# Decays of the sample sequences' states: from VectorE, behind the state sums, to GpSimd, before them

## The chip, the cores and the metric

One core of a Trainium2 chip. The metric is device time in microseconds (us) of one execution, the median of several executions of the same program. Two numbers of a profiled execution come beside it: the span of the trace, and that execution's own device time.

## What is computed

One inference step of a two-layer decoder trunk, for a prompt of 256 tokens and for 8 sample sequences of 4 new tokens each. Each layer projects the normalised input once and feeds three groups of heads: sparse attention with an indexer that picks 256 of 2052 keys (A), dilated window attention (C), and a Mamba-2 scan (B). Their gated outputs are joined and projected back.

What matters here is the recurrent state of B. For each of the 8 sample sequences and 6 heads it is a 64 by 128 matrix, and a step makes of it (cut from the reference):

```python
chunk_decay = jnp.exp(acs[:, :, -1, :])
def step(h, inp):
    st, dec = inp
    return h * dec[:, :, None, None] + st, h
h_final, h_in = lax.scan(step, h0, (states.swapaxes(0, 1), chunk_decay.swapaxes(0, 1)))
```

The old state times its decay, plus the sum over the new tokens. The new state is an output; the token outputs of the layer use the old one.

## The kernel before, in words

Everything lies feature by token: 256 prompt tokens and 32 sample tokens are 288 columns, `T`. The engines run programs of their own, written out by hand in the order in which they issue, and wait on semaphores. A layer has these stages: eight projection tiles; 16 pairs of cache pages with eight more projection tiles between them; the search for the 256th largest score, bit by bit, on VectorE (`compare`, `settle`, 32 rounds) with a small matmul of TensorE in each round (`bit_count`) and projections, the scan and the window attention between the rounds; then the softmax of the sparse attention, 32 groups of value pages (`value_group`) with projections, prompt attention and the state sums between them; then eight output tiles.

**State.** The tile `state` (in the profile `phased`, whose memory it shares) holds the 8 sequences' states, 384 columns each. SyncE loads it (line 501). `sample_offsets` (1368) reads the old states on TensorE. ScalarE writes the decays into `ebc` in `ssd_exp(h)` (836 and 837), once for each of the 6 heads, and counts `ebc_ready`. `state_sums(i)` (1405) puts the new parts of sequences 4i to 4i+3 into PSUM banks, and `state_out(b)` on VectorE (1988) waits for bank `ss{b}`, multiplies the state by the decays (1991), waits for itself, adds the bank (1994) and so gives the bank free. Sequences 0 to 3 are followed by `prompt_state_out` and three `top8_round`, then 4 to 7. GpSimd stores all states once the last bank is free (639).

**GpSimd's program around the change.** After the last rope and its stores come `masked(0)` and `masked(1)` (569), then `consumed(*RING[40:44])`, then `y_gated(t)` for three tiles (590), then `consumed(*RING[44:60])`. `consumed` reloads slots of the ring of eight `kv` buffers: for each item it waits for TensorE to have read the slot and issues four transfers (438), GpSimd for the odd places, SyncE for the even ones. Items 40 to 43 of the ring are window values and items 48 and up are the value pages: `consumed(*RING[40:44])` loads places 49 and 51, and the next call begins with 53 and 55.

**Who waits for `y_gated`.** It multiplies the scan's output by its gate, on a tile whose memory the transposed probabilities take over next. So ScalarE waits for all three before the first exponential of the sparse softmax:

```python
act.wait_ge(S["sexp_in"], nth(L, "sexp_in", 1))
act.wait_ge(S["ki_out"], nth(L, "ki_out", 16))
act.wait_ge(S["y_ready"], nth(L, "y_ready", 3))
sparse_exp(0)
```

These are lines 905 to 908; the exponential itself is line 875. `sexp_in` comes from VectorE (2182), behind the masking of the scores (2174). Behind `sparse_exp` come TensorE's transposes (1006, called at 1501), ScalarE's `sparse_turned` (881), and the value groups.

Of the kernel before, what the change touches and what calls it, by code (L numbers as in the profile page):

```python
# [18 lines left out]
ALU = mybir.AluOpType  # L19
# [8 lines left out]
NB, NQ = 8, 4  # L28
# [72 lines left out]
RING = ([("page", n) for n in range(KITEMS)] + [("window", n) for n in range(2 * NB)] + [("value", n) for n in range(NGRP)])  # L101
# [45 lines left out]
def bank_plan():  # L147
# [59 lines left out]


PER = {
    "rstd_ready": 1, "sq_ready": 8, "sq_used": 5, "y_normed": 5, "y_pooled": 3, "z_gated": 1, "xw_ready": 8, "xn_free": 7, "xn_ready": 8, "roped": 15, "shuffled": 7, "ssum_ready": 1, "root_ready": 1,  # L210
    "qs_ready": 1, "relu_used": 1, "prelu_used": 8, "cnt_ready": NCOUNT + 1, "cin_used": 7, "tanhed": 7, "conved": 7,
    "qz_ready": 1, "qcz_zero": 1, "so_sel": 1, "qcz_ready": 6, "qcbd_ready": 6, "mask_ready": 1, "sexp_in": 1, "sexp": 5, "px_ready": 1,
    "pexp_in": 2, "pexp": 2, "pprob": 2, "pv0_done": 1, "dexp_in": 2, "dexp": 2, "dprob": 2,
# [9 lines left out]
def build(nc, a):  # L223

    plan, _ = bank_plan()
    with ExitStack() as ctx:
        def sb(name, shape, dt=F32):
            return ctx.enter_context(nc.sbuf_tensor(name, shape, dt))
# [52 lines left out]
        state = phasedf.rearrange("p (b n) -> p b n", b=NB)  # L281
# [39 lines left out]
        ebc = sb("ebc", [P, 6, 10])  # L321
# [9 lines left out]
        S = {name: ctx.enter_context(nc.semaphore(name))  # L331
             for name in ("x_in0", "x_in1", "ptab_in", "prm_in", "cst_in", "const_in", "ones_set", "zeroed", "act_chain", "dve_chain", "pool_chain", "y_out",
                          *[f"w_in{n}" for n in range(WSLOTS)], *[f"kv_in{n}" for n in range(NKV)], *PER)}
# [3 lines left out]
        def bank_of(use):  # L337
            return bank[plan[use][0]]

        def filled(use):  # L340
            return S[f"filled{plan[use][0]}"]

        def drained(use):
            return S[f"drained{plan[use][0]}"]

        def nth(layer, what, n=None):

            if n is None:
                what, n = f"filled{plan[what][0]}", plan[what][1] + 1
            return layer * PER[what] + n  # L350
# [38 lines left out]
        def each(ap, m):  # L389

            return ap.unsqueeze(2).to_broadcast([ap.shape[0], ap.shape[1], m])
# [50 lines left out]
        def after(engine, kind, layer, item):  # L442


            at = PLACE[item] + NKV
            layer, at = (layer, at) if at < len(RING) else (layer + 1, at - len(RING))
            if layer < DEPTH and at % 2 == (kind == mybir.EngineType.Pool):
                load_item(engine, kind, layer, at)
# [78 lines left out]
        def _(pool):  # L527
            POOL = mybir.EngineType.Pool
            chain = Chain(S["pool_chain"])
# [4 lines left out]
            for L in range(DEPTH):  # L534
# [14 lines left out]
                def consumed(*items):  # L549

                    for item in items:
                        after(pool, POOL, L, item)
# [14 lines left out]
                def masked(i):  # L567

                    pool.tensor_scalar(xwb[:, i, :], xws[:, 2, :], C("bm", i, i + 1), None,
                                       ALU.mult).then_inc(S["xwb_ready"], 1)  # L570
# [61 lines left out]
                keep(*STAGE_KEEPS[L][4], "proj24")  # L632
                masked(0)
                masked(1)
                consumed(*RING[40:44])
                for t in range(3):
                    y_gated(t)
                consumed(*RING[44:60])
# [963 lines left out]
        def _(dve):  # L1602
# [25 lines left out]
            for L in range(DEPTH):  # L1628
                chain = Chain(S["dve_chain"])
                tt_, ts_, stt = dve.tensor_tensor, dve.tensor_scalar, dve.scalar_tensor_tensor  # L1630
# [357 lines left out]
                def state_out(b):  # L1988

                    dve.wait_ge(filled(f"ss{b}"), nth(L, f"ss{b}"))  # L1990
                    tt_(state[:, b, :].rearrange("p (h n) -> p h n", h=6), state[:, b, :].rearrange("p (h n) -> p h n", h=6),
                             each(ebc[:, :, 2 + b], 64), ALU.mult).then_inc(chain.next(), 1)
                    dve.wait_ge(S["dve_chain"], chain.n)
                    tt_(state[:, b, :], state[:, b, :], bank_of(f"ss{b}")[:, 0:384], ALU.add).then_inc(drained(f"ss{b}"), 1)

                def prompt_state_out():
# [198 lines left out]
                for b in range(4):  # L2195
                    state_out(b)
# [3 lines left out]
                for b in range(4, NB):  # L2200
                    state_out(b)
# [216 lines left out]
```

## Time and profile before

| | us |
|---|---|
| median of 3 executions | 609.94 |
| lowest, highest | 609.93, 610.36 |
| the profiled execution, its own device time | 606.36 |
| span of its trace | 604.6 |

The span is 1.76 us shorter than the profiled execution's own time, which in turn is 3.58 us below the median of the others. Starts are in us from the start of the span. PE is TensorE, DVE VectorE, ACT ScalarE, POOL GpSimd; a number in square brackets behind a timeline row is the idle time of that engine just before it and what ended it. In rows of waits the three numbers are the total in us, how often, and the longest in us; in rows of busy time by stretch, behind the length come TensorE, its weight loads, VectorE, ScalarE and GpSimd, then the granted clock as a share of full speed, the DMA engines' share and GB/s. Layer 0 takes the first 297 us or so, layer 1 the rest; the stretch of the change is at 169 to 222 us and again at 460 to 513 us.

### The profile page before, as it was taken

Reading aid. Unit: us, or ns where it says so; the run is one execution under the profiler, and the core shown is the slowest. Engines: PE = TensorE matmul, PEld = TensorE weight load, DVE = VectorE, ACT = ScalarE, POOL = GpSimd, SP = SyncE. Lnnn points to the kernel's source line nnn. Section 1 sums busy time; section 2 is a strip of 40 time slices with the busy share of each in tenths; the row PEclk is TensorE's granted clock in tenths of the full one; section 3 lists DMA queues with packets and bytes.
Section 4 is the critical chain, followed back from the end, with each engine's and each line's share of the span. In section 5 each row is a group of like instructions: output and inputs, shape, how many; then the busy total and the mean of one; then the engine's idle time right before and its main releaser. Section 6 shows DMA issues by size and latency. Waiting matters only on the chain.

```text
span 604.6 us, 13428 instructions
## 1 busy us (share of the span) xinstructions
PE 555.4 (92%) x4656; PEld 385.6 (64%) x4656; DVE 354.7 (59%) x1081; ACT 175.5 (29%) x457; POOL 241.6 (40%) x433
## 2 busy tenths in 40 slices
PE   4999999999999987999899999999999988799980
PEld 3776655677776654667677565557777755566760
DVE  4864655667776683534267563657678648553223
ACT  3013522112234342641001351311223344264110
POOL 0506642457327446261011474334843464631201
PEclk9999999999999997999999999999999999999996
DMA  8978999999999999798969999999999999993582
GB/s 328 318 279 296 369 368 386 414 355 354 397 395 348 335 307 359 245 347 295 376 208 370 296 362 372 374 417 360 368 367 379 383 336 315 345 322 98 201 302 78
DMA packets 75108, 198.37 MB, mean 328 GB/s; under 512 B 11585, under 2 KB 44770, under 8 KB 70946
## 3 DMA queue, kind: packets, MB, share of 16 engines
q1 hardware_dynamic: 53570, 99.50, 46.7%
q0 software_dynamic: 21472, 98.03, 44.1%
q8 instruction: 37, 0.61, 0.4%
q14 instruction: 29, 0.24, 0.1%
HBM read 189.33 MB, written 52.00 MB: 399 GB/s over the span
## 4 chain that ended last, share of the span: by engine, by line
PE 73%; DMA 9%; DVE 5%; SPq 5%; ACT 5%; issue 2%; DVEq 0%
PE bank L960 69%; DMA kv<-in_kk 6%; SPq L438 4%; PE bank L1006 3%; DMA w<-in_w 3%; ACT shared L765 1%; ACT srow L875 1%; ACT shared L748 1%; DVE shared L1838 1%; DVE shared L1821 1%; DVE st L1827 1%; DVE srow L2174 1%; SPq L434 0%; DVE xn L2256 0%; DVE shared L1785 0%
## 5 line engine op out<-in xcount | busy, mean ns | idle before, releaser
L960 PE MATMUL bank<-xn,w 128*128 128x288 f32 x1120 | 293.8, 416 | 8.2 <-DMA w<-in_w 8.2
L960 PEld LDWEIGHTS bank<-xn,w 128*128 128x128 f32 x1120 | 206.6, 191 | 77.0 <-issue 22.4
L438 POOL DMA_DIRECT2D kv<-in_kk x128 | 68.9, 539 | 91.4 <-PE bank L960 44.2
L438 POOL DMA_DIRECT2D kv<-in_vv x128 | 68.8, 539 | 90.5 <-PE bank L960 49.5
L701 ACT ACTIVATE pt<-bank 128x288 f32<-128x288 f32 x48 | 19.6, 409 | 191.9 <-PE bank L960 191.9
L960 PE MATMUL bank<-pt,w 128*128 128x288 f32 x256 | 64.1, 408 | 1.2 <-DMA w<-in_w 1.2
L960 PEld LDWEIGHTS bank<-pt,w 128*128 128x128 f32 x256 | 48.1, 190 | 15.4 <-DMA w<-in_w 2.0
L541 POOL DMA_DIRECT2D out_keep<-in_buf x48 | 25.0, 527 | 81.1 <-PE bank L960 79.3
L1696 DVE TENSOR_SCALAR_CACHE_REDUCE hit<-sc,tb 128x516 bf16<-128x516 f32 x62 | 46.5, 750 | 2.2
L960 PE MATMUL bank<-kv,qz 128*32 128x256 f32 x512 | 34.3, 385 | 0.0
L960 PE MATMUL bank<-kv,pt 128*32 128x256 f32 x512 | 33.5, 391 | 0.0
L2242 DVE TENSOR_TENSOR x<-x,bank 128x288 f32<-128x288 f32 x16 | 7.3, 454 | 40.0 <-PE bank L960 40.0
L1669 DVE COPY tails<-cin 128x3 f32<-128x3 f32 x14 | 4.8, 344 | 44.1 <-ACT cin L699 41.9
L960 PE MATMUL bank<-pt 64*128 64x128 f32 (+3 forms) x168 | 27.5, 351 | 0.0
L670 ACT ACTIVATE phased<-x 128x288 f32<-128x288 f32 x24 | 10.4, 442 | 58.5 <-DVE x L2242 52.7
L960 PEld LDWEIGHTS bank<-pt 64*128 64x128 f32 (+2 forms) x168 | 18.7, 193 | 11.6 <-issue 10.6
L1675 DVE SCALAR_TENSOR_TENSOR cacc<-cin,prm,cacc 128x312 f32<-128x312 f32 x42 | 22.8, 544 | 1.5
L1707 DVE TENSOR_SCALAR tb<-bank 128x1 int32<-128x1 f32 x62 | 9.6, 155 | 23.8 <-PE bank L960 23.1
L431 POOL DMA_DIRECT2D kv<-in_dil x16 | 8.7, 547 | 35.5 <-PE bank L960 35.3
L960 PEld LDWEIGHTS bank<-kv,pt 128*32 128x32 f32 x512 | 14.4, 111 | 12.1 <-issue 4.7
L960 PEld LDWEIGHTS bank<-kv,qz 128*32 128x32 f32 x512 | 13.4, 109 | 11.8 <-issue 6.3
L960 PE MATMUL bank<-kv,shared 128*32 128x128 f32 x576 | 18.6, 275 | 0.0
(262 smaller groups left out, 737.6 us busy)
## 6 DMA issues: line engine op xcount, KB each, us to landing
w<-in_w SPq DMA_DIRECT2D x86, 512.0 KB, 8.6
out_keep<-in_buf POOLq DMA_DIRECT2D x16, 2044.0 KB, 13.9
kv<-in_kk SPq DMA_DIRECT2D x128, 160.0 KB, 8.4
kv<-in_kk POOLq DMA_DIRECT2D x128, 160.0 KB, 5.8
kv<-in_vv SPq DMA_DIRECT2D x128, 128.0 KB, 4.8
kv<-in_vv POOLq DMA_DIRECT2D x128, 128.0 KB, 4.8
kv<-in_dil SPq DMA_DIRECT2D x16, 576.0 KB, 11.4
kv<-in_dil POOLq DMA_DIRECT2D x16, 576.0 KB, 8.1
```

The lines of the kernel that those rows point to most:

```text
L431: engine.dma_start(kv[:, s, 0:9 * P], a["dil"][layer, item // NB * NB + SEQ_ORDER[item % NB]]).then_inc(S[f"kv_in{s}"], 16)
L438: engine.dma_start(kv[:, s, r * rec:(r + 1) * rec], a["kk" if what == "page" else "vv"][bass.ds(page + layer * N_POOL, 1)].rearrange("o p ...
L541: pool.dma_start(a[f"keep{g}"][bass.ds(layer, 1), b], a[f"buf{g}"][bass.ds(layer, 1), b, 4 * 256:], max_dma_last_dim=COPY_ROW).then_inc(S[ ...
L670: act.activation(squares[:, k % 2, 0:T], x[:, k, :], ACT.Square).then_inc(S["sq_ready"], 1)
L701: act.activation(ptile(i), src[:, 0:T], fn).then_inc(use, 1)
L748: act.activation(psa[:, i, 0:nk], psa[:, i, 0:nk], ACT.Exp, bias=st8[:, 1, i:i + 1], accum_out=st8[:, 2, i:i + 1]).then_inc(S["pexp"] if i ...
L960: return pe.matmul(out, lhsT, rhs, start=start, stop=stop, skip_group_check=True, **k)
L1006: return pe.transpose(out, in_, ident(n))
L1675: stt(out=o, in0=cin[:, n % 2, j:j + COUT], scalar=prmc(L, "cw", 4 * n + j), in1=o, op0=ALU.mult, op1=ALU.add).then_inc(S["cin_used"] if j ...
L1696: ts_(hit[:, :], sc[:, :], old.bitcast(F32), 0.0, ALU.is_ge, ALU.add, accum_out=cnt[:, 0:1]).then_inc(S["cnt_ready"], 1)
L1707: ts_(tb[:, 2:3], src[:, 0:1], float(TOPK_S), float(bit), ALU.is_lt, ALU.mult).then_inc(drained(f"count{n}"), 1)
L2242: tt_(x[:, m, :], x[:, m, :], src[:, 0:T], ALU.add).then_inc(drained(f"out{m}"), 1)
```

## The change

Two places. On GpSimd eight multiplications of a state by its decays are put between `masked(1)` and `y_gated(0)`: four before `consumed(*RING[40:44])`, four behind it, with one wait for the sixth `ebc_ready` ahead of them. On VectorE `state_out` loses its multiplication and the wait for it, and waits for `decayed` instead. Nothing is computed that was not computed before.

```diff
@@ PER
+    "decayed": 8,
@@ GpSimd, layer L
                 masked(0)
                 masked(1)
-                consumed(*RING[40:44])
+                pool.wait_ge(S["ebc_ready"], nth(L, "ebc_ready", 6))
+                for b in range(NB):
+                    if b == 4:
+                        consumed(*RING[40:44])
+                    pool.tensor_tensor(state[:, b, :].rearrange("p (h n) -> p h n", h=6), state[:, b, :].rearrange("p (h n) -> p h n", h=6),
+                                       each(ebc[:, :, 2 + b], 64), ALU.mult).then_inc(S["decayed"], 1)
                 for t in range(3):
                     y_gated(t)
                 consumed(*RING[44:60])
@@ VectorE, state_out(b)
                     dve.wait_ge(filled(f"ss{b}"), nth(L, f"ss{b}"))
-                    tt_(state[:, b, :].rearrange("p (h n) -> p h n", h=6), state[:, b, :].rearrange("p (h n) -> p h n", h=6),
-                             each(ebc[:, :, 2 + b], 64), ALU.mult).then_inc(chain.next(), 1)
-                    dve.wait_ge(S["dve_chain"], chain.n)
+                    dve.wait_ge(S["decayed"], nth(L, "decayed", b + 1))
                     tt_(state[:, b, :], state[:, b, :], bank_of(f"ss{b}")[:, 0:384], ALU.add).then_inc(drained(f"ss{b}"), 1)
```

## Rows read from the trace of the kernel before

**Rows 1.** the page, busy time by engine and granted TensorE clock in 40 slices

```profile
PE 555.4 (92%) x4656; PEld 385.6 (64%) x4656; DVE 354.7 (59%) x1081; ACT 175.5 (29%) x457; POOL 241.6 (40%) x433
...
PEclk9999999999999997999999999999999999999996
```

**Rows 2.** instructions on the tile phased (state), VectorE: ns min/median/max

```profile
L1991 DVE TENSOR_TENSOR phased<-phased,ebc x16: 549/551/559, 206.4 to 511.1; 128x384 f32<-128x384 f32 x16
L1994 DVE TENSOR_TENSOR phased<-phased,bank x16: 553/553/555, 207.0 to 511.6; 128x384 f32<-128x384 f32 x16
```

**Rows 3.** everything TensorE waited for, 190 to 230 us: first and last of 4

```profile
PE bank L1006 <- ACT srow L875: 1.9, 3, 0.7
...
PE bank L1006 <- ACT vtok L741: 0.3, 1, 0.3
```

**Rows 4.** VectorE timeline, layer 0: start us, us, what

```profile
230.46 0.17 DVE L1829 TENSOR_SCALAR st<-st 128x2 f32<-128x2 f32 x1
```

**Rows 5.** ScalarE timeline, both layers

```profile
171.48 0.17 ACT L837 ACTIVATE ebc<-bank 128x8 f32<-128x8 f32 x1
...
231.92 1.28 ACT L765 ACT_TABLE_LOAD   x1
...
484.46 0.72 ACT L875 ACTIVATE srow<-srow,st 128x512 f32<-128x512 f32 x1 [1.86 <-DVE st L2182]
```

**Rows 6.** GpSimd timeline, layer 0: start us, us, what [idle before]

```profile
130.95 2.40 POOL L587 TENSOR_TENSOR xws<-xw,dec 128x384 f32<-128x384 f32 x3
...
184.42 2.32 POOL L438 DMA_DIRECT2D kv<-in_vv  x4 [12.74 <-issue]
187.16 2.29 POOL L438 DMA_DIRECT2D kv<-in_vv  x4 [0.42 <-issue]
189.97 2.30 POOL L594 TENSOR_TENSOR pt<-pt 128x288 f32<-128x288 f32 x3 [0.52 <-ACT pt L902]
192.22 4.27 POOL L438 DMA_DIRECT2D kv<-in_vv  x8
```

**Rows 7.** ScalarE's own wait at line 907: count, ns, first and last start

```profile
L907 ACTq EVENT_SEMAPHORE  x2: 38/38/38, 192.3 to 483.4; - x2
```

**Rows 8.** chain that ended last, layer 0: start us, us, what

```profile
193.46 0.17 DVE st L2182
...
193.65 0.82 ACT srow L875 x2
...
198.60 13.19 PE bank L960 x120
...
277.84 9.81 DMA w<-in_w
```

**Rows 9.** GpSimd timeline, layer 1

```profile
478.01 2.31 POOL L438 DMA_DIRECT2D kv<-in_vv  x4 [0.42 <-issue]
481.08 2.30 POOL L594 TENSOR_TENSOR pt<-pt 128x288 f32<-128x288 f32 x3 [0.75 <-ACT pt L902]
```

**Rows 10.** costliest GpSimd groups by shape: busy us, mean ns

```profile
L569 POOL TENSOR_SCALAR xwb<-xws,const 128x384 f32<-128x384 f32 x4 | 5.0, 1247 | 0.1
...
L654 POOL TENSOR_TENSOR xn<-xn,rstd 128x288 f32<-128x288 f32 x3 | 2.9, 978 | 24.3 <-DVE rstd L1613 24.3
```

**Rows 11.** landing times of the four GpSimd transfers of 192.22 to 194.3 us

```profile
DMA to landing us min/median/max: 4.9/5.1/5.7
```

**Rows 12.** TensorE timeline, layer 1 and layer 0

```profile
489.35 2.80 PE L960 MATMUL bank<-kv,pt 128*32 128x256 f32 x48
...
526.50 0.87 PE L1006 MATMUL bank<-const,shared 128*128 128x128 f32 x6 [3.23 <-DVE shared L1838]
...
235.68 1.54 PE L1006 MATMUL bank<-const,shared 128*128 128x128 f32 x6 [3.23 <-DVE shared L1838]
```

**Rows 13.** one stretch of layer 0: length, busy times, granted clock, DMA share

```profile
236.20:242.00 5.80, 5.80 (x37) 3.33 (x37) 0.80 (x2) 1.15 (x3) 3.13 (x7) 0.54 1.05 377
```

**Rows 14.** VectorE at line 2256, beside line 654: ns min/median/max

```profile
L2256 DVE SCALAR_TENSOR_TENSOR xn<-x,fnw,rstd x5: 503/1037/1046, 593.0 to 596.3; 128x288 f32<-128x288 f32 x5
```

More of the change, by code:

```diff
@@ L209 @@
 PER = {
-    "rstd_ready": 1, "sq_ready": 8, "sq_used": 5, "y_normed": 5, "y_pooled": 3, "z_gated": 1, "xw_ready": 8, "xn_free": 7, "xn_ready": 8, "roped": 15, "shuffled": 7, "ssum_ready": 1, "root_ready": 1,
+    "rstd_ready": 1, "sq_ready": 8, "sq_used": 5, "y_normed": 5, "y_pooled": 3, "z_gated": 1, "decayed": 8, "xw_ready": 8, "xn_free": 7, "xn_ready": 8, "roped": 15, "shuffled": 7, "ssum_ready": 1, "root_ready": 1,
     "qs_ready": 1, "relu_used": 1, "prelu_used": 8, "cnt_ready": NCOUNT + 1, "cin_used": 7, "tanhed": 7, "conved": 7,
```

## The prediction

> **What bounds the kernel now.** The page comes first: TensorE is busy 92% of the span, VectorE 59%, GpSimd 40% [rows 1]. So time taken from VectorE counts only where TensorE stands still for it, and time put on GpSimd only where somebody waits for GpSimd. The question is who waits in the two stretches of the change, and it has to be asked twice, once for what is removed and once for what is added.
>
> **What is removed: worth nothing.** VectorE loses 16 multiplications of 551 ns, eight in each layer, 8.8 us of busy time in all [rows 2]. Between 190 and 230 us TensorE waited four times in kind, every time for ScalarE: for the exponentials, for the squares and roots of the group norm, for evacuated tokens [rows 3]. It never waited for a bank that the states' additions give back, though they came with the multiplications ahead of them. Behind the states VectorE goes through the group norm to the maxima of the dilated scores, done at 230.46 + 0.17 = 230.63 us [rows 4]. The next user is ScalarE's exponential, and ScalarE itself is free only at 231.92, when TensorE's projection has been evacuated [rows 5]. So VectorE is 1.3 us early already, and after the change it is early by 2.2 us more (4 x 0.55, since the first four states and the last four are apart, with waits for TensorE between them). What hides the gain is ScalarE's order behind TensorE; without that cover each layer would gain at most 2.2 us. I take zero.
>
> **What is added, first four.** GpSimd's `masked(1)` ends at 184.42 - 12.74 = 171.68 us [rows 6]. The sixth `ebc_ready` comes from ScalarE's instruction of 171.48 + 0.17 = 171.65 [rows 5]. The new wait costs nothing. Behind it GpSimd is idle for 12.74 us, until TensorE has read the window values and places 49 and 51 can be reloaded. A multiplication has the very form of line 587, 128x384 with the decay broadcast; three of those took 2.40 us one behind the other, so 0.80 each [rows 6]. Four take 3.2 us and end near 175, more than 9 us before the reloads of 184.42. They cost nothing, and no DMA is late for them.
>
> **What is added, last four.** These stand behind the reload of place 51, which ends at 187.16 + 2.29 = 189.45 us, and ahead of `y_gated` [rows 6]. The three `y_gated` start at 189.97 and take 2.30 us; they had waited 0.52 us for ScalarE's gate. With 3.2 us of multiplications in front they start at 192.65 and end at 194.95, where they ended at 192.27.
>
> Who waits for that? ScalarE, at line 907, before the first exponential of the sparse softmax. Its wait there was over at 192.3 and 483.4 us, which is the moment at which `y_gated` ends [rows 7]. The exponential began at 193.65, behind VectorE's instruction of 193.46 + 0.17 = 193.63 [rows 8]. So `y_gated` had 1.38 us to spare in layer 0. Added are 3.20, less 0.52 of idle time filled, less 1.38: the exponential starts 1.3 us later. In layer 1 the reload ends at 478.01 + 2.31 = 480.32; `y_gated` waited 0.75 and ended at 483.38 [rows 9]; the exponential began at 484.46 [rows 5]. So 3.20 - 0.75 - 1.08 = 1.37, 1.4 us. This wait lies on the chain that ended last: exponential, transposes, and from 198.60 on 13.19 us of TensorE without a gap [rows 8]. VectorE's multiplications don't give it back, as they come only after it.
>
> A multiplication's price has two ends. The slowest GpSimd operation on 384 columns, `masked`, took 1.247 us [rows 10]; at that price each layer is 4 x 0.45 = 1.8 us worse. Below 0.77, what `y_gated` needs for 288 columns (2.30 / 3), it can't well go; that saves 0.1 per layer. I take 0.80, the same form in the same engine.
>
> VectorE's own time for the same form is 0.55 [rows 2], so GpSimd is 1.45 times slower. The Trainium skill speaks against such a move (GPSIMD Engine Reference, 4.1 Engine selection: two-input elementwise work belongs on VectorE, GpSimd being about twice as slow; 3.1 gives 1.96 times). An estimate by that figure would be 1.08 us each, and so 2.2 us more for both layers, 4.9 in all. The trace has the duration, so 1.45 stands.
>
> **Behind `y_gated` on GpSimd's queue** stand the reloads of places 53 and 55, which began at 192.22 [rows 6] and now begin near 194.95. Of the four transfers for 53 the last starts 1.6 us later and lands at most 5.7 us after that [rows 11]: at 199.5 before, at 202.3 now. TensorE reads that place in its sixth value group; six groups are 48 matmuls in 2.80 us [rows 12], so the sixth begins 2.3 us after 198.6, at 200.9, and with the delay at 202.2. It is a tie. I take zero here, with up to 0.8 us per layer as the bad end. SyncE's transfers depend on TensorE alone and move with it. The store of the states comes later than all of this and nobody on the chain waits for it. VectorE's new wait for `decayed` is over at 192.7 for the last state, and the first addition comes after 206 [rows 2].
>
> **Does the delay survive?** Near the end of layer 0 TensorE waits 9.81 us for weights [rows 8]. Their load is issued when output tile 0 is done, so it moves with TensorE, and I let the delay through. Layer 1 has no such wait behind the change.
>
> **The sum** is 1.3 + 1.4 = 2.7 us. Against the profiled execution's own 606.36 that is 609.1. The median is 3.58 us above that execution, and I add the sum to it: 609.94 + 2.7 = 612.6.
>
> **Rivals.**
> 1. **The clock.** In the one fall of the granted clock inside the span [rows 1], at 236.2 to 242.0, it was 0.54 over 5.80 us [rows 13], TensorE at its lower level of 1.2 GHz nearly throughout. It lost (1 - 0.54) x 5.8 = 2.7 us. Ahead of it TensorE had stood idle for 3.23 us; in layer 1 the same idle time had no fall behind it [rows 12]. So it is near the edge, and moving the idle times can turn it over. The change also lengthens an idle time, from the 0.7 us before the first transposes [rows 3] to 2.1. One fall more: 612.6 + 2.7 = 615.3, chance 0.12. One fewer: 609.9, no change, 0.11.
> 2. **Faster, by the same mechanism.** The unprofiled executions took 3.58 us more than the profiled one. If a second fall, behind the idle time that ends at 526.50, is part of that, then both falls can go when layer 0's idle time moves by 1.3 and layer 1's by 2.7: 612.6 - 5.4 = 607.2. It decides where neither idle time ends in a fall. For it speaks only that difference; against it, that both must go together. Chance 0.06.
> 3. **Engines in each other's way.** In the last stage three GpSimd multiplications of 288 columns took 978 ns instead of 770 [rows 10], and VectorE's instructions beside them 1037 instead of 503 [rows 14]. If the last four multiplications suffer like that, at 1.25 us each, the time is 612.6 + 3.6 = 616.2. Against it: beside them VectorE adds a PSUM bank to the scores, as it did beside `y_gated`, which ran undisturbed in 2.30 us [rows 6]. Chance 0.05. The Trainium skill has it as an exclusive lock (SBUF, "SBUF: two separate sides"): a VectorE instruction with two SBUF inputs and a GpSimd one that reads SBUF exclude each other. By that rule, the last stage agrees, and the scores' instructions, with one input in PSUM, don't count.
> 4. **Half of it is absorbed**, because the transfers behind layer 0's 9.81 us wait use the delay to land earlier: 611.3, chance 0.06.
> 5. **The change doesn't delay anything**, because the exponential waits for more than I see and `y_gated` has more to spare: 609.9, chance 0.04.
>
> **How the numbers follow.** The forecast, both layers late by 1.3 to 1.4 us, has 0.56; its own range is 612.3 to 614.2 (the tie of place 53 lost in both layers). A measurement of this kernel can tell 0.2% from no change, 1.2 us. Slower by more than that are the forecast, rivals 1 (one more), 3 and 4: 0.56 + 0.12 + 0.05 + 0.06 = 0.79. Within it: 0.11 + 0.04 = 0.15. Faster: 0.06. The range of 609.8 to 615.6 leaves out rivals 2 and 3, 0.11, and edges of the others.
>
> **What would show it.** After the change, ScalarE's first exponential should be released by GpSimd's line of `y_gated`, not by VectorE's line 2182, near 195.0 us and 1.3 us later than before; four multiplications of 0.80 us should lie at 171.7 to 175 and four at 189.5 to 192.7; TensorE's idle time before the first transposes should be 2 us; VectorE should show 8.8 us less busy time and as much more idle time, ended by TensorE and ScalarE. It is wrong if the exponential is still released by VectorE, if TensorE turns out to gain behind 217 us, or if the span moves while the exponentials don't.

## The result, and the profile after

The changed kernel takes 622.67 us (median of 6 runs, 619.60 to 627.91), the kernel before 609.78 in runs beside it (6 runs, 608.29 to 610.36). The ratio is 1.0222, 95% interval 1.0189 to 1.0255: slower by 12.9 us. The forecast was 612.6, with a range up to 615.6: right in sign, about five times too small in size. Medians here are of all executions; ratios and their intervals come from executions taken side by side and leave out those over 1.5% above the fastest of the same kernel, so a ratio isn't always the quotient of two medians. The profiled execution took 627.91 us, with a span of 626.2, so it is the slowest of the six; against the profiled execution of before it is 21.5 us longer, not 12.9.

The page of the changed kernel, busy time by engine and granted clock:

```profile
PE 566.1 (90%) x4656; PEld 391.5 (63%) x4656; DVE 357.8 (57%) x1065; ACT 176.0 (28%) x457; POOL 254.6 (41%) x449
...
PEclk9999999999997997999999999999999897999996
```

GpSimd has its 16 additional instructions and 13.0 us more [rows 1]. But VectorE, which lost 16 multiplications of 0.55 us, is busy 3.1 us *longer*. Something on VectorE has grown by 12 us. The timelines of the stretch in layer 0 show it; GpSimd first (start us, us, what, idle before):

```profile
172.88 3.28 POOL L639 TENSOR_TENSOR phased<-phased,ebc 128x384 f32<-128x384 f32 x4
...
190.38 0.54 POOL L438 DMA_DIRECT2D kv<-in_vv  x1 [0.35 <-issue]
190.93 3.22 POOL L639 TENSOR_TENSOR phased<-phased,ebc 128x384 f32<-128x384 f32 x4
194.12 2.28 POOL L594 TENSOR_TENSOR pt<-pt 128x288 f32<-128x288 f32 x3
```

and VectorE of the changed kernel:

```profile
190.12 0.43 DVE L2170 TENSOR_TENSOR hit<-hit,eqs 128x516 bf16<-128x516 bf16 x1
190.58 5.97 DVE L2172 TENSOR_SCALAR maskbf<-hit 128x516 bf16<-128x516 bf16 x1
```

This is the instruction that turns the result of the search into the additive mask of the scores (line 2169 in the listing of before, where the trace has it so):

```profile
189.43 0.30 DVE L2169 TENSOR_SCALAR maskbf<-hit 128x516 bf16<-128x516 bf16 x1
```

One instruction of 0.30 us takes 5.97, and 6.03 in layer 1. It begins 0.35 us before GpSimd's multiplications and ends at 196.55, 0.15 us after the last `y_gated`: it was shut out while GpSimd worked through all seven instructions (four multiplications, three `y_gated`). GpSimd itself isn't slowed, 3.22 us for four. In the kernel before, the mask began while the last transfer was being issued and ended at 189.73, in the 0.52 us in which GpSimd waited for ScalarE's gate [rows 6].

TensorE waits for the mask, and projects before the softmax only behind it. Its timeline in the changed kernel, layer 0 and layer 1:

```profile
190.26 1.24 PE L965 MATMUL bank<-xn,w 128*128 128x288 f32 x4
196.61 0.62 PE L965 MATMUL bank<-maskbf,bconst 32*128 32x512 bf16 x5 [5.11 <-DVE maskbf L2172]
197.16 5.51 PE L965 MATMUL bank<-xn,w 128*128 128x288 f32 x12
...
206.47 2.80 PE L965 MATMUL bank<-kv,pt 128*32 128x256 f32 x48
...
496.05 0.62 PE L965 MATMUL bank<-maskbf,bconst 32*128 32x512 bf16 x5 [5.16 <-DVE maskbf L2172]
496.60 5.97 PE L965 MATMUL bank<-xn,w 128*128 128x288 f32 x12
```

The same stretch before:

```profile
189.11 1.24 PE L960 MATMUL bank<-xn,w 128*128 128x288 f32 x4
190.28 0.40 PE L960 MATMUL bank<-maskbf,bconst 32*128 32x512 bf16 x5
190.61 3.18 PE L960 MATMUL bank<-xn,w 128*128 128x288 f32 x12
...
198.53 2.80 PE L960 MATMUL bank<-kv,pt 128*32 128x256 f32 x48
```

From the four matmuls to the value groups it was 198.53 - 189.11 = 9.42 us and is 206.47 - 190.26 = 16.21: 6.8 us more. In layer 1 it is 7.3 more. Three terms: the wait, 5.1 us; twelve matmuls at a lower granted clock, 5.51 instead of 3.18, 2.3 us; and 0.7 us less waiting for the exponentials, which now lie beside the slow projection. Both layers give 14.1 us. The rest of the 21.5 is mostly further falls of the clock: in the last 120 us, from the value groups of layer 1 on, the granted clock was 0.91 where it had been 0.95, and that stretch is 4.6 us longer. The two PEclk rows show them (2 slices under nine tenths before, the last one among them, and 5 after), and they differ from execution to execution. The changed kernel was profiled once more (e9_after_again): 618.56 us in that execution, 12.2 above the profiled one of before, and there the two stretches come to as much. Its TensorE timeline in layer 0:

```profile
191.55 1.24 PE L965 MATMUL bank<-xn,w 128*128 128x288 f32 x4
197.88 0.62 PE L965 MATMUL bank<-maskbf,bconst 32*128 32x512 bf16 x5 [5.10 <-DVE maskbf L2172]
198.43 4.86 PE L965 MATMUL bank<-xn,w 128*128 128x288 f32 x12
...
207.09 2.80 PE L965 MATMUL bank<-kv,pt 128*32 128x256 f32 x48
```

207.09 - 191.55 = 15.54, so 6.1 more than before; in layer 1 it was 5.9 more, together 12.0.

Last, what the forecast rested on. ScalarE's exponential in the changed kernel:

```profile
200.20 0.72 ACT L880 ACTIVATE srow<-srow,st 128x512 f32<-128x512 f32 x1 [7.25 <-DVE st L2185]
```

It is still released by VectorE, which the prediction had named as a sign of being wrong. `y_gated` ended at 196.40, which is 5.5 us behind the last transfer issue where it had been 2.8: 2.7 us later, as forecast. But the exponential was not due before 200.20.

### The profile page after: what moved, and what is told of

Read it like the earlier page. It is cut to its first block and busy times, and to the rows that moved or that the text cites. A ratio compares the mean times of both kernels' runs of the same rounds, so it can differ in the third digit from the quotient of the medians.

```text
span 626.2 us, 13440 instructions
## 1 busy us (share of the span) xinstructions
PE 566.1 (90%) x4656; PEld 391.5 (63%) x4656; DVE 357.8 (57%) x1065; ACT 176.0 (28%) x457; POOL 254.6 (41%) x449
## 5 line engine op out<-in xcount | busy, mean ns | idle before, releaser
L965 PE MATMUL bank<-xn,w 128*128 128x288 f32 x1120 | 299.6, 422 | 8.1 <-DMA w<-in_w 8.1
L965 PEld LDWEIGHTS bank<-xn,w 128*128 128x128 f32 x1120 | 210.3, 195 | 80.5 <-issue 23.9
L965 PE MATMUL bank<-kv,pt 128*32 128x256 f32 x512 | 35.6, 411 | 0.0
L675 ACT ACTIVATE phased<-x 128x288 f32<-128x288 f32 x24 | 10.4, 441 | 58.9 <-DVE x L2245 53.4
L965 PE MATMUL bank<-kv,ea 64*32 64x128 f32 x512 | 14.4, 281 | 5.2 <-DMA kv<-in_kk 4.0
```

Of the source, the lines that this page charges most:

```text
L675: act.activation(squares[:, k % 2, 0:T], x[:, k, :], ACT.Square).then_inc(S["sq_ready"], 1)
L965: return pe.matmul(out, lhsT, rhs, start=start, stop=stop, skip_group_check=True, **k)
```

## The experiments

All ratios are to the kernel before on the same chip. Its medians there were 609.37 us (17 runs) beside e1 to e4, 610.28 (23 runs) beside e5 to e7 and 608.98 (11 runs) beside e8 and e9. A kernel with one run is told with the one run of before beside it.

**e1_gaps: the same order, but with pauses.** Each of the last four multiplications waits for its predecessor's semaphore.

```diff
                     if b == 4:
                         consumed(*RING[40:44])
+                    if b >= 4:
+                        pool.wait_ge(S["decayed"], nth(L, "decayed", b + 1))
```

> The changed kernel, but GpSimd waits on its own count behind each of the last four multiplications, so that no two of its instructions there follow each other without a pause. Theory G (VectorE's bf16 mask instruction, 0.30 us before and 5.97 us after the change, can't begin as long as GpSimd runs instructions back to back, and begins at the first pause): it ends behind the first multiplication, within 1.2 us of its start; TensorE's wait for it (5.1 and 5.2 us) falls below 0.9 us; what is left is the late y_gated, so 612.5 to 614 us. Rival H (the mask instruction shares its time with GpSimd's instructions for as long as these run, pauses or not): it still lasts over 5 us and the time is that of the changed kernel, 619 to 628 us.

The wait is for the count that the multiplication ahead has given. Measured: 616.21 us (6 runs), ratio 1.0144 [1.0098, 1.0190]. Instructions on the tile `maskbf` and TensorE's timeline:

```profile
L2174 DVE TENSOR_SCALAR maskbf<-hit x2: 1357/1389/1421, 189.7 to 482.4; 128x516 bf16<-128x516 bf16 x2
```

```profile
196.96 1.95 PE L1013 MATMUL bank<-const,srow 128*128 128x128 f32 x8 [2.38 <-ACT srow L882]
```

The four multiplications took 3.60 instead of 3.22 us, and the mask got in behind the first of them: 1.4 us instead of 6. So it isn't the multiplications beside it that cost the time, but that there is no pause between them. With the mask out of the way, the forecast's own delay appears: 2.4 us of idle time before the first transposes, where there were 0.7.

**e2_all_early: all eight ahead of the reload.** Nothing is added between the transfers and `y_gated`.

```diff
                 for b in range(NB):
-                    if b == 4:
-                        consumed(*RING[40:44])
                     pool.tensor_tensor(state[:, b, :]...
...
+                consumed(*RING[40:44])
```

> The changed kernel, with all eight multiplications ahead of the reload of ring places 49 and 51, in GpSimd's idle 12.7 us. Theory G and the prediction's late y_gated both expect nothing left: the multiplications end near 178.5 us (layer 0), the mask takes 0.30 us, y_gated starts when ScalarE's gate is done, and the time is that of the kernel before, 609 to 611 us. A theory by which the states' multiplications on GpSimd cost time wherever they stand (or VectorE's additions without them do) expects 615 us or more.

Measured: 610.76 (12 runs), 1.0045 [1.0017, 1.0073]. The mask is back at 0.29 us. GpSimd and VectorE in the early stretch:

```profile
172.75 6.47 POOL L637 TENSOR_TENSOR phased<-phased,ebc 128x384 f32<-128x384 f32 x8
```

```profile
173.50 1.74 DVE L2047 TENSOR_TENSOR dx<-drow,const 128x32 f32<-128x32 f32 x3
```

VectorE's small instructions are held here too, but briefly: three take 1.74 us, 0.39 before. Nearly the whole loss is gone. Of the 0.45% that is left, TensorE's waits show 0.9 us, two waits for VectorE's rounds of the search, which the kernel before doesn't have; the rest isn't explained. VectorE is spared 8.8 us of multiplications and the kernel isn't faster.

**e3_mask_first: the last four only after the mask.**

```diff
                     if b == 4:
                         consumed(*RING[40:44])
+                        pool.wait_ge(S["mask_ready"], nth(L, "mask_ready", 1))
```

> The changed kernel, but GpSimd begins the last four multiplications only when VectorE's mask is written (one more wait). It leaves the order on GpSimd and so the late y_gated as in the changed kernel. Theory G: mask 0.30 us, TensorE's 5 us wait gone, and what is left is the prediction's own term, the exponential 1.5 to 1.7 us late in each layer behind y_gated: 612.5 to 613.5 us. If the late y_gated cost nothing by itself, 610 us; if the loss were not in the mask, 619 us or more.

Measured: 615.19 (6 runs), 1.0106 [1.0046, 1.0165]; the mask takes 0.30 us. TensorE's timeline:

```profile
195.91 1.97 PE L1012 MATMUL bank<-const,srow 128*128 128x128 f32 x8 [2.53 <-ACT srow L881]
...
200.86 3.64 PE L966 MATMUL bank<-kv,pt 128*32 128x256 f32 x48
```

This is the forecast's mechanism by itself: 2.53 us idle instead of 0.73, 1.8 more in a layer, where the forecast had 1.3 to 1.4. Behind it the value groups take 3.64 instead of 2.80 us, and 4.72 in layer 1: in this profile the granted clock fell behind the longer idle time in both layers. From the mask's matmuls to the end of the value groups the profile has 3.6 us more in layer 0 and 4.2 in layer 1, of which 1.8 each is the idle time; the medians differ by 5.8. So the forecast's own mechanism, with the mask out of the way, costs about twice the 2.7 us of the forecast; rival 1 of the prediction had one such fall with a chance of 0.12.

**e4_extra: four other multiplications in the old kernel.** VectorE keeps its multiplications; GpSimd gets four that compute nothing that is used, from other tiles, ahead of `y_gated`.

```diff
                 consumed(*RING[40:44])
+                pool.wait_ge(S["xwb_ready"], nth(L, "xwb_ready", 2))
+                pool.wait_ge(S["roped"], nth(L, "roped", 15))
+                for out, n in ((xws[:, 2, :], 384), (pt[:, 3, :], T), (tmp[:, :], T), (rstd[:, :], T)):
+                    pool.tensor_tensor(out, xw[:, 2, 0:n], xw[:, 1, 0:n], ALU.mult)
```

> The kernel before, VectorE's program unchanged, with four added GpSimd multiplications ahead of y_gated whose results nobody reads (384, 288, 288 and 288 columns, 3.1 us in all). Theory G: the mask instruction is held until the run of seven ends, about 5.8 us, TensorE waits about 5 us in each layer, and the time is that of the changed kernel, 619 to 628 us, with no state involved. Rival K (the loss comes from the states' tile, or from the new counts and waits between the engines): about 612 us, the late y_gated alone.

Measured: 622.50 (4 runs), 1.0273 [1.0198, 1.0348]. Tile `maskbf`:

```profile
L2173 DVE TENSOR_SCALAR maskbf<-hit x2: 5685/5862/6039, 189.8 to 485.0; 128x516 bf16<-128x516 bf16 x2
```

The whole loss, without the change: the states, `ebc` and VectorE's relief have no part in it.

**e5_two_inputs and e8_two_inputs_late: another form of the mask.** Is it only the fast form with one bf16 input that is shut out? In e5 the mask is made from two tiles (rounded in bf16, so the mask of the chosen keys isn't exactly zero there):

```diff
-                tt_(hit[:, :], hit[:, :], eqs[:, :], ALU.add).then_inc(chain.next(), 1)
+                ts_(eqs[:, :], eqs[:, :], -NEG, NEG, ALU.mult, ALU.add).then_inc(chain.next(), 1)
...
-                ts_(maskbf[:, :], hit[:, :], -NEG, NEG, ALU.mult, ALU.add).then_inc(S["mask_ready"], 1)
+                stt(out=maskbf[:, :], in0=hit[:, :], scalar=-NEG, in1=eqs[:, :], op0=ALU.mult, op1=ALU.add).then_inc(S["mask_ready"], 1)
```

> The changed kernel, GpSimd's program unchanged. VectorE builds the mask with an instruction of two SBUF inputs, and the one-input bf16 step (times 1e30, less 1e30) is done one instruction earlier, before GpSimd's run begins. Theory G1 (only an instruction of one input in VectorE's fast form is shut out for the whole run; one with two inputs gets in between two GpSimd instructions, as line 2048's three did beside the first four multiplications, 1.04 us instead of 0.39): the mask ends within 1.7 us, TensorE waits less than 1.3 us for it, the late y_gated stays: 613 to 617 us, as with the pauses. Theory G2 (every VectorE instruction that reads SBUF twice at once is shut out until the run ends): mask about 5.5 us, 619 to 628 us.

Measured: 613.99 (12 runs), 1.0068 [1.0036, 1.0099]. The mask took 0.69 us, but it began at 189.91, 0.07 us into the last transfer issue, where the changed kernel's began 0.20 us into it. So the form and the moment have changed together, and it doesn't tell the forms apart. GpSimd gave way here, if only a little: its four multiplications took 3.31 us in both layers, against 3.22. It shows the late `y_gated` once more: 2.53 us idle before the first transposes.

In e8 the same order as in the changed kernel is kept, with a second operand, one column spread over the tile (`below`, filled once with -2^99; the mask's large value is 2^99 instead of 1e30):

```diff
-                ts_(maskbf[:, :], hit[:, :], -NEG, NEG, ALU.mult, ALU.add).then_inc(S["mask_ready"], 1)
+                stt(out=maskbf[:, :], in0=hit[:, :], scalar=2.0 ** 99, in1=below[:, 0:1].to_broadcast([P, SEG]), op0=ALU.mult, op1=ALU.add).then_inc(S["mask_ready"], 1)
```

> The changed kernel, GpSimd's program unchanged, and VectorE's mask instruction in the place where it was, but with two SBUF inputs (the marks and a column broadcast along the row; the constant is 2 to the power 99 instead of 1e30). It starts about 0.35 us ahead of GpSimd's first late multiplication, as the shut-out instruction of the changed kernel did, and reaches into the run. Theory G1 (only the one-input fast form is shut out for the whole run): it ends within 1.7 us, TensorE waits less than 1 us for it, and the time is that of the runs with pauses, 613 to 617 us. Theory G2 (any instruction that reads SBUF through both ways is shut out until the run ends): about 6 us, TensorE's wait stays at 5 us, 619 us or more.

Measured: 622.38 (6 runs), 1.0178 [1.0110, 1.0247]:

```profile
L2174 DVE SCALAR_TENSOR_TENSOR maskbf<-hit,below x2: 6362/6395/6428, 191.4 to 484.5; 128x516 bf16<-128x516 bf16 x2
```

The slow form with two inputs is shut out just as long. Between these two forms, the form doesn't decide.

**e6_behind_gate: the last four behind `y_gated`.**

```diff
-                for b in range(NB):
-                    if b == 4:
-                        consumed(*RING[40:44])
+                for b in range(4):
...
+                consumed(*RING[40:44])
                 for t in range(3):
                     y_gated(t)
+                for b in range(4, NB):
+                    pool.tensor_tensor(state[:, b, :]...
```

> The changed kernel, with the last four multiplications behind the three y_gated instead of ahead of them. GpSimd then pauses between the reload and y_gated, where VectorE writes its mask. Theory G and the late y_gated both expect their loss to be gone: mask 0.30 us, the exponential released by VectorE. What is left is the delay of the reloads of places 53 and 55 by 3.2 us, against which the value groups no longer move: TensorE waits up to 2 us for place 53 in each layer if its slack is as small as the prediction had it. 609.5 to 613 us.

Measured: 611.59 (12 runs), 1.0018 [0.9985, 1.0052]: no difference. GpSimd's timeline:

```profile
189.00 0.63 POOL L438 DMA_DIRECT2D kv<-in_vv  x1 [0.35 <-issue]
189.75 2.29 POOL L594 TENSOR_TENSOR pt<-pt 128x288 f32<-128x288 f32 x3
192.01 3.22 POOL L643 TENSOR_TENSOR phased<-phased,ebc 128x384 f32<-128x384 f32 x4
195.19 4.27 POOL L438 DMA_DIRECT2D kv<-in_vv  x8
```

The mask (189.21, 0.30 us) again goes through beside the last transfer issue. It came 0.21 us into it, as in the changed kernel (0.20); the difference is that `y_gated` was not ready yet. GpSimd paused only 0.12 us behind the issue, in both layers. Its neighbours then are VectorE's instructions with a PSUM bank as input, which run undisturbed (0.69 and 0.68 us, as before). The reloads of 53 and 55 begin 3 us later than before. In layer 0 nobody waits for them; in layer 1 TensorE does, for 0.17 us, behind 40 matmuls of the value groups and so just ahead of the sixth group, where the prediction had its tie:

```profile
492.67 0.64 PE L967 MATMUL bank<-kv,pt 128*32 128x256 f32 x8 [0.17 <-DMA kv<-in_vv]
```

So with a little more than the forecast's delay the tie is all but kept. And VectorE's 8.8 us are worth nothing again.

**e7_two_late: two instead of four behind the transfers** (`if b == 6` in place of `if b == 4`).

> The changed kernel, with six multiplications ahead of the reload and two behind it. The run in front of VectorE's mask is now five GpSimd instructions, 1.6 + 2.3 us. Theory G: the mask is held for that run, about 4.2 us in all, TensorE waits 3.3 to 3.6 us in each layer. y_gated ends before the exponential needed it in the kernel before, so nothing of the prediction's late y_gated is in it, and the whole loss is the mask's: 615 to 620 us. If the loss were that y_gated is late, 610 us.

Measured: 616.97 (6 runs), 1.0129 [1.0076, 1.0181]. Tile `maskbf`, and TensorE's timeline:

```profile
L2172 DVE TENSOR_SCALAR maskbf<-hit x2: 4376/4404/4432, 190.0 to 489.4; 128x516 bf16<-128x516 bf16 x2
```

```profile
194.41 0.62 PE L965 MATMUL bank<-maskbf,bconst 32*128 32x512 bf16 x5 [3.51 <-DVE maskbf L2172]
```

The run is then two multiplications and three `y_gated`, 1.65 + 2.27 us. The mask takes as long as the run plus what it was early: 4.4 us for five instructions, 6.0 for seven.

**e9_after_again: the changed kernel once more**, beside e8.

> The changed kernel itself, beside the one above on the same chip, as the yardstick for it: mask instruction near 6 us in both layers, TensorE's wait for it 5.1 us in each, 619 to 628 us.

Measured: 619.39 (4 runs), 1.0171 [1.0115, 1.0228]; mask 5.96 and 6.03 us, TensorE's wait 5.1 and 5.2.

**e10_mask_early: the mask's form inside the early run.** In e2, a second mask instruction (its result is overwritten later) stands on VectorE behind the window probabilities, where GpSimd's run of eight lies beside it.

```diff
+                dve.wait_ge(S["cnt_ready"], nth(L, "cnt_ready", 27))
+                ts_(maskbf[:, :], hit[:, :], -NEG, NEG, ALU.mult, ALU.add).then_inc(chain.next(), 1)
```

> The kernel with all eight multiplications early, plus one more mask instruction (the same bf16 form with one input, its result overwritten later) in VectorE's program right behind window_probs, so that it falls into GpSimd's run of eight, at about 174 to 176 us. Theory F (the form of VectorE's instruction decides: 516 bf16 elements are shut out until a run ends, the small float32 ones of line 2048 slip in between two instructions): it lasts until the run's end, some 3 to 5 us. Theory D (the place decides: shut out for a whole run is what begins while GpSimd still issues a transfer directly ahead of the run): it waits for one GpSimd instruction, 1.2 us at most.

Measured: 619.59 in the one run (611.70 before). GpSimd's and VectorE's timelines:

```profile
171.51 6.52 POOL L637 TENSOR_TENSOR phased<-phased,ebc 128x384 f32<-128x384 f32 x8
```

```profile
173.99 0.91 DVE L2139 TENSOR_SCALAR maskbf<-hit 128x516 bf16<-128x516 bf16 x1
```

The same instruction, inside a longer run of the same multiplications, waits for one of them and not for all. Where the run stands decides, not what VectorE executes. The one time is no good measure of cost: TensorE waited 2.0 us in all for the rounds of the search there, 0.9 in e2, and the granted clock was 0.971 against 0.979.

**e11_mask_inside: the mask 0.8 us later.** In the changed kernel a comparison of 0.75 us is put ahead of the mask (its result is not used), so that the mask begins inside the late run and not beside the transfer issue.

```diff
+                ts_(eqs[:, :], sc[:, :], bound, 0.0, ALU.is_equal, ALU.add, accum_out=cnt[:, 1:2]).then_inc(chain.next(), 1)
+                dve.wait_ge(S["dve_chain"], chain.n)
                 ts_(maskbf[:, :], hit[:, :], -NEG, NEG, ALU.mult, ALU.add).then_inc(S["mask_ready"], 1)
```

> The changed kernel, with VectorE's comparison for equal scores made a second time directly ahead of the mask instruction (0.75 us, a form that was never held up), so that the mask instruction begins inside the run instead of 0.35 us ahead of it. Theory F: it is shut out until the run's end all the same, about 5 us, and TensorE's wait stays near 5 us. Theory D: it gets in between two GpSimd instructions, 1.2 us at most, and TensorE waits about 1.5 us.

Measured: 625.24 in the one run (611.70 before). GpSimd and VectorE:

```profile
190.49 0.54 POOL L438 DMA_DIRECT2D kv<-in_vv  x1 [0.35 <-issue]
191.04 3.23 POOL L639 TENSOR_TENSOR phased<-phased,ebc 128x384 f32<-128x384 f32 x4
194.23 2.28 POOL L594 TENSOR_TENSOR pt<-pt 128x288 f32<-128x288 f32 x3
```

```profile
191.51 5.15 DVE L2174 TENSOR_SCALAR maskbf<-hit 128x516 bf16<-128x516 bf16 x1
```

It began 0.47 us into the run and was still held to its end. So it isn't that it arrived during the transfer issue. The comparison itself, which began 0.32 us before the run and reaches into it, wasn't held.

**e12_transfers_ahead: transfers put ahead of the early run.** In e10, three transfers that GpSimd issues ahead of `masked(0)` (the copies of line 541, `keep`) are moved behind `masked(1)`.

```diff
-                keep(*STAGE_KEEPS[L][4], "proj24")
                 masked(0)
                 masked(1)
+                keep(*STAGE_KEEPS[L][4], "proj24")
                 pool.wait_ge(S["ebc_ready"], nth(L, "ebc_ready", 6))
```

> The kernel of e10_mask_early (all eight multiplications in one run behind the masked tiles, with an additional mask instruction beside them) with one thing moved: GpSimd's three transfers that copy finished outputs (line 541), which stood ahead of the masked tiles, are issued directly ahead of the run of eight. Nothing else changes; every multiplication of the run is free to start when the transfers have been issued, as in the late place. Theory H (transfers that GpSimd issues directly ahead of a run make it hold VectorE out until the run has no ready instruction left): the three comparisons of line 2048 or the additional mask, whichever comes first inside the run, takes until the run's end, so 3 to 6 us in place of 0.9 to 1.7, in both layers, and the additional mask follows with 0.30 us; TensorE then waits several us for the counts of the search, and the time is over 620 us. Theory I (the transfers ahead have nothing to do with it; the late place differs in something else): as in e10, the comparisons take 1.0 to 1.8 us for three, the additional mask 0.86 to 0.91 us, and the time is 612 to 620 us.

Measured: 613.45 in the one run (608.33 before). GpSimd and VectorE:

```profile
168.71 1.62 POOL L541 DMA_DIRECT2D out_keep<-in_buf  x3 [0.68 <-PE bank L964]
172.81 6.52 POOL L637 TENSOR_TENSOR phased<-phased,ebc 128x384 f32<-128x384 f32 x8 [2.48 <-ACT ebc L841]
```

```profile
175.29 0.91 DVE L2139 TENSOR_SCALAR maskbf<-hit 128x516 bf16<-128x516 bf16 x1
...
177.22 0.61 DVE L1974 TENSOR_TENSOR cs<-ea,pt 128x128 f32<-128x128 f32 x1
```

As in e10. But between the transfers and the run GpSimd had waited 2.48 us for the decays, which the late place does not have. So this says what a pause does, and not yet what transfers do without one.

**e13_no_pause: the same without the pause.** The wait for the decays and the first multiplication now stand ahead of the three transfers, seven multiplications directly behind.

```diff
-                keep(*STAGE_KEEPS[L][4], "proj24")
                 pool.wait_ge(S["ebc_ready"], nth(L, "ebc_ready", 6))
                 for b in range(NB):
+                    if b == 1:
+                        keep(*STAGE_KEEPS[L][4], "proj24")
```

> The kernel of e12_transfers_ahead, in which the three transfers were issued behind the masked tiles but a wait of 2.48 us for the decays lay between them and the run of eight, so that it did not have what the late place has: a multiplication that is ready the moment the transfer issue ends. Here the first multiplication stands ahead of the three transfers and seven stand directly behind them, with nothing to wait for. Theory H (transfers directly ahead, with no pause, make GpSimd hold VectorE out until nothing ready is left): the first bf16 or f32 SBUF instruction of VectorE that falls on the run of seven (a comparison of line 2048, the additional mask, or the product of line 1975) takes until the run's end, 3 to 5.6 us, and the profile shows no other pause of GpSimd to end it. Theory I (the transfers have nothing to do with it, even without a pause): none of them takes over 1.7 us, and those beside the run 0.6 to 0.9 us, as in e10 and e12. The time: over 618 us by H, 612 to 618 by I.

Measured: 621.21 in the one run (609.61 before). GpSimd's timeline, VectorE's, and TensorE's waits:

```profile
171.45 0.84 POOL L638 TENSOR_TENSOR phased<-phased,ebc 128x384 f32<-128x384 f32 x1 [4.77 <-ACT ebc L842]
172.24 1.64 POOL L541 DMA_DIRECT2D out_keep<-in_buf  x3
173.90 5.66 POOL L638 TENSOR_TENSOR phased<-phased,ebc 128x384 f32<-128x384 f32 x7
```

```profile
172.58 0.33 DVE L2140 TENSOR_SCALAR maskbf<-hit 128x516 bf16<-128x516 bf16 x1
...
174.28 4.59 DVE L1975 TENSOR_TENSOR cs<-ea,pt 128x128 f32<-128x128 f32 x1
...
470.77 4.59 DVE L1975 TENSOR_TENSOR cs<-ea,pt 128x128 f32<-128x128 f32 x1
```

```profile
PE bank L965 <- DVE hit L1701: 8.1, 2, 4.0
```

The loss has been made in another place, with another VectorE instruction. The product of line 1975 (1974 in e12) takes 0.28 us alone and 0.61 beside the runs of e10 and e12; beside this run it takes 4.59 in both layers, into the last multiplication (it ends at 178.87, the run at 179.56). TensorE then waits 4.0 us in each layer for VectorE's next round of the search. The mask and the three small products of line 2048 (the expectations call them comparisons), beside the transfer issue with only a transfer as GpSimd's next instruction, weren't held.

## Why the prediction was wrong in size

**What the runs settle.** VectorE is shut out for (nearly) a whole run of GpSimd instructions where the run stands directly behind transfers that GpSimd issues, with every instruction ready. It is let in behind a single instruction where the run stands behind other work (`masked`, in e2 and e10) or behind a pause (e12), or has waits in it (e1). The pair e12 and e13 shows both ends: with the 2.48 us pause the product takes 0.61 us, without it 4.59. Each of the two is one execution, but both layers of each agree. In the late place e1 (1.4 us), e7 (4.4) and the changed kernel (6.0) agree, and so does the undisturbed mask of the kernel before, of e3 and of e6: there GpSimd's next instruction was not ready when the mask came, if only by 0.12 us (e2 and e6). One case doesn't fit a rule as short as this: e5's mask, 0.13 us earlier in the transfer issue and of another form, was let through with the run ready behind it. Why a transfer issue has this effect stays open, and so does how few transfers it takes for a long run.

**The kernel before has it too, on a small scale.** In layer 1 GpSimd issues one transfer and clears a tile directly behind it; VectorE's instruction of line 1742 begins during the issue and ends with the clearing:

```profile
397.19 0.53 POOL L431 DMA_DIRECT2D kv<-in_dil  x1 [2.66 <-PE bank L960]
397.70 0.60 POOL L561 MEMSET vtok<- 128x576 f32 x1
```

```profile
397.36 1.02 DVE L1742 TENSOR_SCALAR iacc<-iacc 128x128 f32<-128x128 f32 x1
```

In layer 0 the same instruction begins at 106.20, 0.01 us ahead of its transfer issue, and takes 0.23 us. The 15 profiles of this case have 30 such places. Where it began before the issue or in its first 0.01 us (13 of them), it took 0.23 us; where it began 0.04 us or more into the issue (13) or beside the clearing (4), it was held until the clearing was over, 0.27 to 1.16 us. So one transfer is enough to hold VectorE over the one instruction that is ready behind it, and the prediction could have read the hold, and with it the price of a wrong moment, in the trace that it had.

**By its steps.**

- *Removed: worth nothing.* Held. e2 and e6 take all 8.8 us from VectorE and are not faster (1.0045 and 1.0018).
- *First four: free.* Held for the stretch before the reload: 3.28 us at 172.88, and the reload isn't late for them. That they hold VectorE's small instructions was not seen: 1.04 us instead of 0.39 for the three of line 2048. TensorE showed no wait for that in the changed kernel.
- *Last four: `y_gated` late, exponential 1.3 to 1.4 us later.* The mechanism is right and was measured alone in e3, at 1.8 us in a layer, and with it a fall of the clock in both layers. In the changed kernel it didn't show, as the exponential was kept for longer by the mask. So that the sign was right is luck: the loss came by another path.
- *"Who waits for that? ScalarE, at line 907".* This is the step that failed. It asked who waits for GpSimd's result, and that has one answer. It did not ask who needs GpSimd to be idle. The mask of line 2169 lay at 189.43 to 189.73, beside the last transfer issue and GpSimd's 0.52 us of waiting, and the prediction had that idle time as a gain ("less 0.52 of idle time filled").
- *Rival 3, engines in each other's way.* The right kind of mechanism, with a chance of 0.05 and a time of 616.2. It was argued away with VectorE's instructions beside the run that read PSUM; those do run undisturbed. The one that reads and writes SBUF alone stands 1.3 us ahead of them and was overlooked. The price was also taken on the wrong side: what suffers is not GpSimd's multiplication (0.80, as forecast, not 1.25) but VectorE's instruction, and through it TensorE, 5.1 and 5.2 us. The prediction took from the Trainium skill (SBUF — State Buffer, "SBUF: two separate sides") that a VectorE instruction with two SBUF inputs and a GpSimd one exclude each other; by that part of the rule the mask, which has one, would not have counted. The section also names VectorE's fast two-port mode, which the prediction left out, and says that the loser waits for the whole instruction of the other. The trace has it shut out for 5.97 us, and e8's form with two for 6.40. That is seven instructions' length and not one's, so the rule, even in full, gives the 0.9 us of e10 and not the loss.
- *The clock, one fall more, 2.7 us, 0.12.* Too low. Behind the 5.1 us of idle time the twelve matmuls took 5.51 and 5.97 us instead of 3.18 in one profile and 4.86 and 4.55 in the other: 1.4 to 2.8 us in each layer. Rival 1's idle time, 2.1 us before the first transposes, wasn't there in the changed kernel; where it was, in e1, e3 and e5, a lower clock followed in both layers.
- *Place 53 is a tie, zero.* Held: in e6, with more delay than forecast, TensorE waits for it 0.17 us in one layer and not in the other.
- *"TensorE waits 9.81 us for weights".* Misread: 9.81 us is how long the load took. TensorE stands idle for it for 1.16 us, as its timeline before the change shows below. The sum doesn't hang on it, but rival 4, which lets half of the 2.7 us vanish in that wait, had only these 1.16 us to take them from.

```profile
287.70 4.62 PE L960 MATMUL bank<-pt,w 128*128 128x288 f32 x17 [1.16 <-DMA w<-in_w]
```

**The sum as it should have been**, by the second profile: 5.1 + 5.2 us of waiting for the mask, 1.7 + 1.4 for the projection at a lower clock, and about -0.7 in each layer because the exponentials then lie beside that projection: 12.0 us. Measured were 12.9 and, in the repetition, 10.4 (619.39 - 608.98).

No version here is faster than the kernel before; the best, e6, is equal to it.

## What to carry to other kernels

Before work is put on GpSimd, read what VectorE does in the same microseconds, and not only who waits for GpSimd's result: a short VectorE instruction in SBUF that feeds TensorE can be held for as long as GpSimd has work ready, if that work stands directly behind transfers it issues. Such a run wants a real wait ahead of it, one that isn't over yet when VectorE's instruction comes, or waits between its instructions, or a place beside VectorE instructions that read PSUM. And a VectorE busy time that goes up when instructions were taken away points at once to a held instruction: look for the form whose mean has grown.

## What the runs showed of the hardware that was not expected

- One VectorE instruction of 0.30 us was held for 5.97 us, over seven GpSimd instructions; GpSimd's pace was the same, 0.80 us each for 384 columns.
- Within one transfer issue the moment decided: begun 0.01 us into it, line 1742's instruction took 0.23 us; begun 0.04 us into it, 1.16.
- Held: bf16 with one input (5.97), bf16 with two inputs (6.40), f32 with two inputs (4.59 instead of 0.28), f32 with one input (1.02 instead of 0.23). Not held: instructions with a PSUM bank as input, the search for maxima and their replacement (`MAX8`, `MATCH_REPLACE8`, 0.43 and 0.41 us inside the run of e3, as before), and the comparison with accumulation of 0.75 us, which also read an f32 tile in SBUF and reached into the run in e11.
- Idle times of 2.4 to 2.6 us in front of the transposes were followed by matmuls at a lower granted clock in both layers of e1, e3 and e5 (48 matmuls in 3.45 to 4.72 us instead of 2.80). It isn't the idle time alone: in layer 0 of e6, behind 0.7 us, they took 3.33.
